# Routing of a mixture of experts on one core: router products on the unnormalised rows, the first pair's indices made on the engines, and two loads held back

## The reference, cut to what matters

```python
x = x + gt1[:, None, :] * y                        # y: the mixer's output projection
h = modulate(rmsnorm(x, g_norm2), sh2, sc2)        # rmsnorm(x) * (1 + sc2) + sh2
y = hierarchical_moe(h, w_rg, b_rg, w_re, b_re, w_e_gate, w_e_up, w_e_down)

def hierarchical_moe(h, ...):                      # 512 tokens, 4 groups of 8 experts
    p_grp = softmax(h @ w_rg + b_rg)               # top-1 group
    le = (h @ w_re + b_re).reshape(T, 4, 8)        # logits of the experts in it
    top_p, top_e = top_k(softmax(le_sel), 2)       # top-2 experts of that group
    w_tok = p_g * top_p / sum(top_p)
    # the rows of each expert go through (silu(x @ gate) * (x @ up)) @ down, and
    # each token sums its two results with w_tok
```

## Time and profile before

| | us |
|---|---|
| median of three runs | 2403.06 |
| the profiled execution, its device time | 2400.21 |
| its span | 2398.5 |

### The profile page before, as it was taken

How to read it: one execution, slowest core, us unless ns; L and a number is a source line. 1 busy time by engine, 2 the same in 40 slices (tenths; PEclk the granted TensorE clock), 3 DMA queues, 4 the chain that set the end, 5 groups by cost and what they waited for, 6 DMA issues and landing times.

```text
span 2398.5 us, 29687 instructions
## 1 busy us (share of the span) xinstructions
PE 2199.6 (92%) x11694; PEld 1570.2 (65%) x11694; DVE 1198.9 (50%) x1768; ACT 751.3 (31%) x1232; POOL 118.2 (5%) x160
## 2 busy tenths in 40 slices
PE   7999998679999999888994989999999899999997
PEld 3788657433333333356784977888887687888885
DVE  4899575400000000158657345777625563877822
ACT  3222442311111111234553334223324363222421
POOL 0000000021111111100003000000000000000000
PEclk9999999889999999989997699999999899999999
DMA  9442205549999999721110011222223101222221
GB/s 388 163 176 96 74 6 210 211 164 405 404 415 404 401 415 405 296 87 70 70 71 1 2 71 71 105 105 82 93 106 141 71 1 71 106 105 88 87 105 70
DMA packets 35350, 384.53 MB, mean 160 GB/s; under 512 B 9024, under 2 KB 9280, under 8 KB 12352
## 3 DMA queue, kind: packets, MB, share of 16 engines
q1 hardware_dynamic: 27520, 374.89, 39.5%
q0 software_dynamic: 7744, 8.44, 1.0%
HBM read 381.85 MB, written 14.73 MB: 165 GB/s over the span
## 4 chain that ended last, share of the span: by engine, by line
PE 59%; DMA 9%; DVE 5%; ACT 3%; issue 3%; POOL 0%; POOLq 0%; SPq 0%; ACTq 0%; DVEq 0%
PE PS L628 14%; PE PS L629 14%; PE PS L630 14%; DMA A<-h_tokens,idx 8%; PE PS L868 5%; PE PS L830 2%; PE PS L875 1%; PE PS L820 1%; PE PS L998 1%; ACT A L1433 1%; PE PS L913 1%; PE PS L588 1%; PE PS L823 1%; PE PS L1191 1%; DVE A L1840 0%
## 5 line engine op out<-in xcount | busy, mean ns | idle before, releaser
L629 PE MATMUL PS<-h_r,w_hi_r 128*128 128x512 f32 x1104 | 432.3, 392 | 0.0
L628 PE MATMUL PS<-h_hi_r,w_hi_r 128*128 128x512 f32 x1056 | 423.8, 401 | 8.5 <-DVE A L1840 3.0
L630 PE MATMUL PS<-h_hi_r,ring_r 128*128 128x512 f32 x1056 | 412.6, 391 | 0.0
L2121 DVE TENSOR_TENSOR ring_r<-ring,w_hi_r 128x1024 fp32r<-128x1024 f32 x196 | 238.7, 1222 | 343.1 <-ACT w_hi_r L1443 342.8
L1443 ACT ACTIVATE w_hi_r<-ring 128x1024 fp32r<-128x1024 f32 x196 | 206.2, 1058 | 564.2 <-PE PS L630 330.8
L628 PEld LDWEIGHTS PS<-h_hi_r,w_hi_r 128*128 128x128 f32 x1056 | 199.4, 189 | 62.8 <-issue 10.5
L629 PEld LDWEIGHTS PS<-h_r,w_hi_r 128*128 128x128 f32 x1104 | 209.2, 190 | 47.4 <-issue 5.2
L630 PEld LDWEIGHTS PS<-h_hi_r,ring_r 128*128 128x128 f32 x1056 | 199.4, 189 | 42.1
L2110 DVE TENSOR_TENSOR A<-A,PS 128x512 f32<-128x512 f32 x16 | 11.0, 688 | 386.9 <-PE PS L830 386.9
L830 PE MATMUL PS<-A 128*64 128x512 f32 x768 | 169.8, 599 | 0.1
L1840 DVE SCALAR_TENSOR_TENSOR A<-A,vec 128x511 f32<-128x511 f32 (+15 forms) x216 | 160.1, 741 | 6.7
(11 more groups left out here) (448 smaller groups left out, 3440.0 us busy)
## 6 DMA issues: line engine op xcount, KB each, us to landing
A<-wexp SPq DMA_DIRECT2D x64, 2048.0 KB, 12.7
ring<-wall SPq DMA_DIRECT2D x63, 2048.0 KB, 8.1
ring<-wexp SPq DMA_DIRECT2D x16, 2048.0 KB, 19.0
h<-wexp SPq DMA_DIRECT2D x16, 2048.0 KB, 19.0
A<-wada SPq DMA_DIRECT2D x12, 2048.0 KB, 14.9
x<-xt_in SPq DMA_DIRECT2D x2, 2048.0 KB, 10.7
A<-y_assignments SPq DMA_DIRECT2D x4, 1024.0 KB, 7.9
h_tokens<-A SPq DMA_DIRECT2D x4, 512.0 KB, 2.8
```

The lines of the kernel that those rows point to most:

```text
L628: mm(out, w[0], x_[0], start=first, stop=False)
L629: mm(out, w[0], x_[1], start=False, stop=False)
L630: return mm(out, w[1], x_[0], start=False, stop=last_)
L2121: tt(ring_r[:, slot, :, cols], ring[:, slot, :, cols], w_hi_r[:, :, cols].bitcast(F32), ALU.subtract).then_inc(S("w_lo"), 1)
```

## The change

Before the last output tile (p = 7), PE multiplies the shift's product with the router weights (one product), the router weights scaled by gm with x tiles 0 to 5, and sums of squares of tiles 0 to 3; the rest of both follows behind p = 7. POOL makes the scaled weights `wg` and the shift's product `wshift` earlier, from "gT_ev" on. ACT squares each tile of x as soon as it is finished. The factor per token (`rstdT`) is worked out on four columns of 128 tokens. The rows of x are transposed instead of those of h, and get the factor at their eviction; gain and shift are put on the gathered rows at their eviction, which takes sixteen ACTIVATEs instead of two for each pair. h is no longer made. The indices of pair 0 come from twelve small products of a one-hot comparison of ranks with token numbers. POOL gathers pair 0 first, then fills the slot table. SP issues the loads of down 1 and gate 3 only when the first gather has landed.

```diff
@@ sync
             down_of(0, wexp[0:1])
-            gate_of(1, 1, wexp[3:4])
             for t in range(NT):
                 sp.wait_ge(S("ht_ev"), t + 1)
                 sp.dma_start(f_tok[t * P:(t + 1) * P, :], ...).then_inc(S("f_tok"), 16)
-            sp.wait_ge(S("logits"), 2)
+            for j in range(2):
+                sp.wait_ge(S(f"xg{j}"), 16)
             down_of(1, wexp[1:2])
+            gate_of(1, 1, wexp[3:4])
@@ tensor
+            def router_logits(ks):
+                for k in ks:
+                    pe.wait_ge(S("xt"), k + 1)
+                    last = mm(PS[HALF * (k % 2):HALF * (k % 2 + 1), 4, :], wg[:, k, :], x[:, k, :], ...)
+            def square_sums(ks):
+                for k in ks:
+                    g = QUARTER * (k % 4)
+                    pe.wait_ge(S("sq"), sq_count(1) + k + 1)
+                    last = mm(PS[g:g + QUARTER, 5, :], ones[:, 0:QUARTER], x2[k], ...)
             for p in range(KD):
+                if p == KD - 1:
+                    pe.wait_ge(S("wg"), 5)
+                    pe.wait_ge(S("xt"), KD - 2)
+                    mm(PS[:, 7, 0:NG + E], ones, wshift[:, 0, 0:NG + E], ...).then_inc(S("logits"), 1)
+                    router_logits(range(KD - 2))
+                    square_sums(range(4))
...
+            router_logits(range(KD - 2, KD)).then_inc(S("logits"), 1)
+            square_sums(range(4, KD)).then_inc(S("logits"), 1)
+            pe.wait_ge(S("rexp"), 1)
+            for t in range(NT):
+                last = mm(PS[:, 6, 64 * t:64 * t + NG + E], lgT[:, t * P:(t + 1) * P], both[:], ...)
+            last.then_inc(S("logits"), 1)
+            pe.wait_ge(S("rg"), 1)
+            for t in range(NT):
+                last = mm(PS[:, 7, 64 + t:65 + t], sums_q[:, t * P:(t + 1) * P], ones[:, 0:1], ...)
             last.then_inc(S("logits"), 1)
@@ behind the rank products
-            n = doubles(pe)
+            pe.wait_ge(S("rg"), 4)
+            for t in range(NT):
+                for lo, n, e, bank in ((0, HALF, 0, 5), (HALF, HALF, 1, 5), (P, QUARTER, 0, 4)):
+                    last = mm(PS[lo % P:lo % P + n, bank, 0:2], onehot[:, t, lo:lo + n], C("mine")[...], ...)
+            last.then_inc(S("rank"), 1)
             rows_T(16)
+            n = doubles(pe)
@@ scalar
+            act.wait_ge(S("logits"), 2)
+            a_(lgT, PS[:, 4, :], ACT.Copy).then_inc(S("rexp"), 1)
+            act.wait_ge(S("logits"), 5)
+            inv_sqrt(rstdT[:], PS[:, 7, 64:64 + NT], 0, 1.0 / (QUARTER * D)).then_inc(S("std"), 1)
             for t in range(NT):
                 act.wait_ge(S("ht_mm"), t + 1)
+                a_(A[:, 40 + 2 * t:42 + 2 * t, :], PS[...], ACT.Identity, scale=rstdT[:, t:t + 1])
...
             def rows_out(count):
                 act.wait_ge(S("m_tr"), count)
-                a_(x_main, PS[:, 0:2, :], ACT.Copy).then_inc(S("m_x"), 1)
+                for k in range(KD):
+                    cols = slice((k % 4) * P, (k % 4 + 1) * P)
+                    last = a_(x_main[:, k // 4, cols], PS[:, k // 4, cols], ACT.Identity, bias=mod[:, 24 + k:25 + k], scale=gm[:, 1, k:k + 1])
+                # x_rest likewise: eight of 128 x 32 in place of one of 128 x 256
@@ vector
-            norm(1, gm[:, 1, :], h, "h_pre")
+            dve.wait_ge(S("logits"), 3)
+            cp(sums_q, PS[:, 5, :]).then_inc(S("rg"), 1)
-            dve.wait_ge(S("logits"), 2)
+            dve.wait_ge(S("logits"), 4)
+            dve.wait_ge(S("std"), 2)
+            link(tt(lg, PS[:, 6, 0:256]..., b3(rstdT[:], NG + E), ALU.mult))
+            link(tt(lg, lg, rbias[:]..., ALU.add))
...
+            link(stt(key, rank[:, :, 0:2], 1.0, asg[2][:, :, 0:2], ALU.add, ALU.mult))
+            tt(onehot[:, :, 0:P]..., C("iotar")..., key..., ALU.is_equal)
+            link(tt(onehot[:, :, P:PAIR_ROWS], ..., ALU.is_equal))
+            nc.vector.memset(er[3], 1.0).then_inc(S("rg"), 1)
...
             link(tt(asg[3], rank, by_expert(er[3]), ALU.add))
+            dve.wait_ge(S("rank"), 2)
+            tt(idx[:, 0, 0, :], PS[:, 5, 0:2], C("nobody"), ALU.add).then_inc(S("posi"), 1)
+            tt(idx[0:QUARTER, 0, 1, :], PS[0:QUARTER, 4, 0:2], ...).then_inc(S("posi"), 1)
@@ gpsimd
+            pool.wait_ge(S("gT_ev"), 1)
+            # wshift = wrt * shift, three halving adds, wg = wrt * gain
+            pool.wait_ge(S("f_tok"), 16 * NT)
             for j in range(2):
-                places(0, 0, j)
+                pool.wait_ge(S("posi"), j + 1)
+                gather(0, j)
+            for c in range(2):
+                pool.wait_ge(S("posi"), c + 3)
+                # the four scatters of choice c
+            for c in range(2):
+                pool.wait_ge(S(f"sc{c}"), 16 * NT)
             for j in range(2):
-                rwait(pool, S(f"idx{j}"), 16)
-                gather(0, j)
                 places(1, 1, j)
```

More of the change, by code:

```diff
@@ L141, in used_count @@
 def used_count(n):
-    return sum(2 if i in GROUPED else KD for i in range(n))
+    return sum(2 if i in GROUPED else KD if i != 1 else 0 for i in range(n))
 def split_count(u, j):
@@ L215, in build @@
         both = sb("both", [P, NG + E])
+        rbias = sb("rbias", [P, NG + E])
+        wg = wif
+        x2 = [A[:, 40 + k, :] for k in range(KD)]
         tok = sb("tok", [P, 8, 2], I32)
@@ L794, in tokens_T @@
                 for k in range(KD):
-                    last = nc.tensor.transpose(PS[:, 2 + 2 * (t % 2) + k // 4, (k % 4) * P:(k % 4 + 1) * P], h[:, k, t * P:(t + 1) * P], ident)
+                    last = nc.tensor.transpose(PS[:, 2 * (t % 2) + k // 4, (k % 4) * P:(k % 4 + 1) * P], x[:, k, t * P:(t + 1) * P], ident)
                 last.then_inc(S("ht_mm"), 1)
-            tokens_T(0)
-            pe.wait_ge(S("eps"), 8)
-            pe.wait_ge(S("rexp"), 1)
             for t in range(NT):
-                last = mm(PS[:, 0, 64 * t:64 * t + NG + E], lgT[:, t * P:(t + 1) * P], both[:], start=True, stop=True)
-            last.then_inc(S("logits"), 1)
-            for t in range(1, NT):
                 tokens_T(t)
@@ L1390, in _ @@
                 a_(merged_hi(k), A[:, 24 + k, :], ACT.Copy).then_inc(S("h_hi"), 1)
-            for p in range(2, 8):
-                last_w_hi(p)
-            norm(1)
             for k in range(KD):
[L1395 to L1399, removed]
+                if k + 2 < KD:
+                    last_w_hi(k + 2)
@@ L1411, in rows_out @@
                 act.wait_ge(S("m_tr"), count)
-                a_(x_main, PS[:, 0:2, :], ACT.Copy).then_inc(S("m_x"), 1)
+                for k in range(KD):
+                    cols = slice((k % 4) * P, (k % 4 + 1) * P)
+                    last = a_(x_main[:, k // 4, cols], PS[:, k // 4, cols], ACT.Identity, bias=mod[:, 24 + k:25 + k], scale=gm[:, 1, k:k + 1])
+                last.then_inc(S("m_x"), 1)
                 act.wait_ge(S("m_tr"), count + 1)
-                a_(x_rest, PS[:, 2, 0:KD * QUARTER], ACT.Copy).then_inc(S("m_x"), 1)
+                for k in range(KD):
+                    cols = slice(k * QUARTER, (k + 1) * QUARTER)
+                    last = a_(x_rest[:, cols], PS[:, 2, cols], ACT.Identity, bias=mod[:, 24 + k:25 + k], scale=gm[:, 1, k:k + 1])
@@ L1416, in _ @@
+                last.then_inc(S("m_x"), 1)
             rows_out(1)
+            n = doubles(act)
             with act.Fori(0, n) as d:
@@ L2046, in _ @@
             tt(asg[2], asg[0], asg[1], ALU.add).then_inc(S("asg"), 1)
+            mine = C("mine").rearrange("p (a e c) -> p a e c", e=2, c=2)[:, :, :, 1]
+            link(tt(mine, mine, asg[1][:, :, 0:2], ALU.add))
             def by_expert(v):
```

86 lines of the change are left out of this document (56 added, 30 removed).

## The result

The changed kernel takes **2382.96 us** (median of 4 runs, 2378.8 to 2384.57), the kernel before beside it 2402.16 (4 runs, 2396.84 to 2407.78): a ratio of 0.9912 with a 95% interval from 0.9889 to 0.9934. 2378.5 was forecast, 2370 to 2389 as range. A second comparison on another chip gave 2380.79 and 0.9911 [0.9881, 0.9941]. So some 19 to 21 us are gained where 24.5 were forecast: the sign and the range were right, and the gain came out a fifth smaller than forecast.

What follows compares the result with a forecast made beforehand. Bound: the weight stream, restarted by "m_pc" 3. Gains of 25.9 us by PE's start after the gather, less 2.0 for eviction, plus 0.5 for clock, give 24.4: 2400.21 to 2375.8, plus 2.85 for the runs' median, 2378.5; range 2370 to 2389.

Steps and rivals of the forecast that it cites:

- What bounds the kernel: Expert loop lives on the weight stream; the date of "m_pc" 3 moves the loop and all behind it, 24.4 us earlier.
- The rival that it doesn't do what it says: Restart not following "m_pc" 3, or a missed wait tying gather to slot table: 2399; missed wait given 0.04.
- Work ahead of tile 7, and the logits: Router work before the last output tile adds 3.8 us; logits then finish at 450.85, 8.8 gained.
- Indices: Pair 0's indices ready at 463.15; one-hot products on PE taken as 2.2 us, dear end at low clock 5.8.
- Gather: Pair 0's gather issued at 463.9 and 465.3, landed 2.2 later; PE starts at 467.5, 25.9 us gained.
- ACT's eviction: Pair 0's main rows, eight two-pointer operations: 3.05 us for 1.03, so 2.0 lost, bounds 1.0 to 2.9.
- The clock of the first products: Pair 0's products start later after PE wakes, so fewer run slow: 0 to 2.0 us gained, 0.5 taken.
- the rival of the low clock: Ranks, one-hot products and transposes at half speed cost 4.6 us: 2383; inside the forecast case's 0.80.
- Held loads: Two 2 MB loads after the first gather, from 467.5 to 478, cost nothing; slot scatters land by 478 to 480.
- Pair 1's rows: Second gather lands by 487, wanted at 492, margin 5; rival: late gather loses about 12 us, 2390, chance 0.09.
- ACT in the loop: Row evictions grow from 1.4 to 5.5 us a pair, hidden in ACT's waits; rival: ACT takes loop, 2441, chance 0.04.
- Loop length unchanged within 4: From line 455 to the end of the last line 875, the loop keeps its length within 4 us.

Runs made afterwards that it cites:

- e_table: Changed kernel with pair 0's indices made through the table of slots again, router part and held loads kept: 2396.09 us, ratio 0.9975.
- the repeated after: The changed kernel again, unedited, with a second trace on another chip: 2380.79 us.
- e_warm: Changed kernel plus unused products on PE around ranks, one-hot products and first transposes: 2383.56 us, ratio 0.9923.
- e_nohold: Changed kernel with the two held loads back at their old places, not waiting for the first gather: 2387.27 us, ratio 0.9937.
- e_delta: Changed kernel with one POOL wait moved in the second block's decay stage, so POOL's product follows DVE's small copy: 2377.85 us, ratio 0.9899.
- e_plain: Changed kernel with gain and shift left out of the gathered rows' evictions (plain copies, part of the computation missing): 2377.32 us, ratio 0.99.
- e_double: Changed kernel with each of the sixteen row evictions run twice, once into unused columns: 2390.05 us, ratio 0.9939.

## Why the prediction was right, and where it was off

Dates of after are given on the clock of before, 2.65 later than its trace has them.

- **What bounds the kernel.** Right. SP's restart follows "m_pc" 3 by 0.06 us, and where it moved by much the end moved with it (e_table: 16.05 and 15.3 against the repeated after). For moves of 2 to 4 us the scatter of the loop is too large to see it. The rival that it doesn't do what it says falls with this.
- **Work ahead of tile 7, and the logits.** Right to 0.6: residual ended at 446.1 (forecast 445.65), logits done at 451.4 (450.85), ranks at 458.95 (458.35).
- **Indices.** 463.5 for 463.15. The term that had no row, twelve one-hot products, took 2.10, for 2.2; but by another reason. They ran at the lower clock, where my dear end was 5.8; at the higher they take 1.54 (e_warm). The bounds of the price were too wide and the value taken was lucky.
- **Gather.** Issued at 464.4 and 466.0 (463.9 and 465.3). PE wakes at 468.35 for 467.5: **0.85 lost in sum**. 0.46 of it is there at the first issue, from the dates before. 0.2 comes from the spacing of 1.30, taken from a row of scatters in full flow: the first indirect DMA takes 1.33 itself, and the second starts 1.63 behind it. The last 0.2 is the landing, 2.36 for 2.2.
- **ACT's eviction.** 2.90 for 3.05 on the main rows: the step from one pointer to two, by two rows of other shapes, was good to 5%. Main and rest rows of a pair together take 5.1 for 5.5; for the rest rows (2.30) no row of before had a price.
- **The clock of the first products.** The mis-sized term. I took a gain of 0.5, by the thought that PE's products come later after its waking; they took 16.83 and 15.52 in the two traces, 15.86 before. So the term, taken as +0.5, was worth -1.0 and +0.3 in the two, and the rival of the low clock (2383) was partly true: e_warm prices the low clock in this stretch at 3.1 to 4.0. The sum: 24.4 - 0.85 - 1.4 = 22.2, which is the measured one.
- **Held loads.** "Cost nothing" is right for the restart (e_nohold: they bring 2 us). Their end was the weak step: forecast 478, the data moved until 480 on after's own clock, some 482.6 on before's, and the slot scatters were seen at 484.2 where 478 to 480 was forecast. The index read took 2.26 more. Small scatters did not pass the loads: 6.95 to 8.46 us after the last issue in the six traces with both loads held and the slot table beside them, 1.77 to 2.40 in the four with one of them held or none.
- **Pair 1's rows.** Margin 5 forecast, 2 and 0.7 measured, and in e_delta, with the same routing code, the rows are 1.36 late. In after's own trace PE waits for nothing at 491.48, so the rival fell there, but not by the margin that was claimed; where it strikes it costs 1.4 at that place and not 12. As the limit of what can still be gained there it is real, as e_plain and e_warm show.
- **ACT in the loop.** Right: hidden, with 4.1 to 4.8 us of ACT's idle left in a pair (forecast about 4), and e_double shows where the cover ends.
- **Loop length unchanged within 4.** It scattered by 2.6 us in the two traces of before and by 5.0 in the two of after, with the clock of the down products. I had allowed 4 for the phase; that was a little small.
- **Missed altogether:** the decay stage behind the loop. I had taken the time behind the restart as a block that only shifts. In the traces of after it is 2.6 to 2.7 longer, of 2.6 to 3.2 for all behind the loop, and that alone is more than the errors in the routing stretch (2.2 and 1.4).

With the medians: 22.6 (mean of the pairs in the stretch) - 2.9 (rest) = 19.7, and the loop as it falls; 19.2 was measured against before in the one comparison, 19.9 in the other (2400.65 - 2380.79).

## What to carry to other kernels

A path that goes through memory only to have its indices sorted is worth looking at: one comparison of ranks with a ramp and twelve narrow products gave 16 of the 23 us here. After a bound is moved, look at once for the next arrival: a margin of 5 us on paper was 2 in one trace, 0.7 in the next and gone in a third. Take such a margin from several traces, not from one. And don't treat the work behind the change as rigid: compare stage lengths between the two traces, since a stage whose engines meet in another order can change by more than the term that you are arguing about.

## What was unexpected in the hardware

- Eight indirect scatters of POOL, of 8 bytes a row, issued beside two loads of 2 MB, were seen only behind the end of the loads: 6.95 to 8.46 us after the last, and 1.77 to 2.40 where at most one such load was issued beside them and was over by then.
- A DVE copy of 8 columns takes 1.47 or 1.77 us instead of 0.16 when a POOL product of 2.35 us has started before it, and ends within 0.03 us of it.
- With unused products in PE's waits the clock still fell for a while (0.50 and 0.65 in 462 to 466), but was back at the first transposes and products: 13.96 for 15.52 to 16.83 us of the same 32 products (64 records), and 1.04 for 1.94 for eight transposes.
- Eight evictions from PSUM with two pointer operands: 2.90 us at 128x128 and 2.30 at 128x32. The quarter of the data saves a fifth of the time.
